# Seven block products in place of eight for the two first matrices of a feed-forward, with tokens stationary and the activations turned

## What is computed

```
h = rmsnorm(x, norm_ffn_g[layer])
x = x + (silu(h @ w1) * (h @ w3)) @ w2      # w1, w3: 1024 x 2816, w2: 2816 x 1024
```

## Time and profile before

| | |
|---|---|
| median of three runs | 2030.04 us |
| span of the profiled execution | 2026.6 us |
| TensorE matmul busy | 1956.4 us (97%) |
| TensorE weight load busy | 1243.3 us (61%) |
| VectorE busy | 466.4 us (23%) |
| ScalarE busy | 324.9 us (16%) |
| HBM read | 561.97 MB, 278 GB/s over the span |

### The profile page before, as it was taken

The page is one execution under the profiler, slowest core; times in us unless marked ns, Lnnn a source line. Parts: engine busy times, 40 slices in busy tenths (PEclk is TensorE's granted clock), DMA queues, the critical chain, the costliest instruction groups (busy, mean ns, idle before and its releaser), DMA issues.

```text
span 2026.6 us, 25597 instructions
## 1 busy us (share of the span) xinstructions
PE 1956.4 (97%) x10149; PEld 1243.3 (61%) x10150; DVE 466.4 (23%) x886; ACT 324.9 (16%) x686; POOL 28.9 (1%) x50
## 2 busy tenths in 40 slices
PE   7999899999999999999999999999999999999998
PEld 4866444433334444433333348788888899888887
DVE  1441311111011111101101123541101377410102
ACT  1231211111011111111101123421000120210001
POOL 2200000000000000000000000000000000000000
PEclk8999899999999999999999999999999999999999
DMA  9959499999989979999999996334444433344410
GB/s 354 307 184 376 185 395 421 422 422 422 422 337 420 421 311 420 422 422 422 422 421 422 422 351 199 104 105 145 160 151 147 144 113 110 118 140 160 150 42 22
DMA packets 170668, 563.94 MB, mean 278 GB/s; under 512 B 10758, under 2 KB 110376, under 8 KB 118128
## 3 DMA queue, kind: packets, MB, share of 16 engines
q1 hardware_dynamic: 167648, 554.96, 71.0%
q0 software_dynamic: 2192, 7.34, 1.3%
q10 hardware_dynamic: 768, 0.76, 0.1%
HBM read 561.97 MB, written 1.05 MB: 278 GB/s over the span
## 4 chain that ended last, share of the span: by engine, by line
PE 79%; DMA 14%; SPq 4%; DVE 1%; ACT 1%; issue 1%; DVEq 0%
PE psum L1173 15%; PE psum L809 15%; DMA ring<-in_w_dram 13%; PE psum L837 8%; PE psum L1145 7%; PE psum L1206 5%; PE psum L952 5%; SPq L418 4%; PE psum L659 4%; PE psum L588 3%; PE psum L780 2%; PE psum L796 2%; PE psum L1227 1%; PE psum L818 1%; DMA ring<-in_w_ada_dram 1%; PE psum L565 1%
## 5 line engine op out<-in xcount | busy, mean ns | idle before, releaser
L809 PE MATMUL psum<-ring,arena 128*64 128x512 f32 x2176 | 490.8, 596 | 38.4 <-DMA ring<-in_w_dram 38.4
L809 PEld LDWEIGHTS psum<-ring,arena 128*64 128x64 f32 x2176 | 151.9, 137 | 369.5 <-issue 252.8
L1173 PE MATMUL psum<-hT,ring 128*128 128x256 f32 x1408 | 307.5, 379 | 0.0
L1173 PEld LDWEIGHTS psum<-hT,ring 128*128 128x128 f32 x1408 | 267.5, 190 | 36.4
L837 PE MATMUL psum<-ring,arena 128*64 128x512 f32 x1088 | 241.7, 597 | 3.2
L1973 DVE TENSOR_SCALAR arena<-psum 128x512 f32<-128x512 f32 x34 | 23.5, 692 | 731.7 <-PE psum L818 731.7
L837 PEld LDWEIGHTS psum<-ring,arena 128*64 128x64 f32 x1088 | 77.7, 137 | 145.4 <-issue 145.4
L1145 PE MATMUL psum<-arena,ring 128*128 128x256 f32 x640 | 141.4, 379 | 0.0
L1145 PEld LDWEIGHTS psum<-arena,ring 128*128 128x128 f32 x640 | 121.6, 190 | 16.5
L1444 ACT ACTIVATE arena<-arena 128x512 f32<-128x512 f32 x34 | 21.4, 630 | 547.2 <-DVE arena L1973 547.1
L1206 PE MATMUL psum<-hT,ring 128*128 128x256 f32 x352 | 79.1, 379 | 0.0
(11 more groups left out here) (388 smaller groups left out, 1617.5 us busy)
## 6 DMA issues: line engine op xcount, KB each, us to landing
ring<-in_w_dram SPq DMA_DIRECT2D x384, 1024.0 KB, 22.6
ring<-in_ffn_w_dram SPq DMA_DIRECT2D x66, 1024.0 KB, 5.3
ring<-in_w_ada_dram SPq DMA_DIRECT2D x24, 1024.0 KB, 11.2
ring<-in_odd_w_in_dram SPq DMA_DIRECT2D x16, 1024.0 KB, 5.5
ring<-in_even_w_in_dram SPq DMA_DIRECT2D x13, 1024.0 KB, 12.7
ring<-in_w_in_dram SPq DMA_DIRECT2D x12, 1024.0 KB, 17.8
ring<-in_w_out_dram SPq DMA_DIRECT2D x4, 1024.0 KB, 14.7
ring<-in_even_w_out_dram SPq DMA_DIRECT2D x4, 1024.0 KB, 5.1
```

The costliest lines, as they stand in the source:

```text
L809: mm = nc.tensor.matmul(bank[4 + q][64 * h:64 * h + 64, :], xg[:, k, SLOTS * r:SLOTS * (r + 1)], ring[(C_MOE + k) % RING][:, (2 * h + q) * ...
L1173: mm = nc.tensor.matmul(bank[4 + 2 * (i % 2) + b][:, h * T:(h + 1) * T], cols(n)[:, k, h * P:(h + 1) * P], hT[:, k * T:(k + 1) * T], start ...
```

## The change

Let the 256 tokens be two blocks of 128 (rows of the product) and the 1024 channels two halves; w1's chunk is one column block of the weights, w3's the other, so a step is a product of a 2x2 by a 2x2 of blocks. It is now formed by Winograd's form of Strassen's algorithm, with seven products of blocks (`p1` to `p7`) where eight stood. With A11, A12 the halves of the first 128 tokens, A21, A22 of the second, and B11, B21 those of w1, B12, B22 of w3:

- four sums of activations, once a feed-forward, into the dead `mixT` (`ffn_x`): A21+A22, that less A11, A11-A21, A12 less the second;
- four sums of weights, in every step, 128x1024 each (`split_weights`): T1 = B12-B11, T2 = B22-T1, T3 = B22-B12, T4 = B21-T2, into one of two sets of buffers (`ffn_w`);
- seven products of 4 matmuls. The stationary operand is a 128x128 block of activations and 256 columns of weights (from the ring or `ffn_w`) move, so results have tokens as rows. P1 lies in bank 4, and ScalarE copies it (`ffn_kept`) before P2 is added in the same bank; P6, P7 and P4 add up in bank 5, P5 and P3 in bank 6;
- VectorE reads the banks between the products and adds P1 and its own sums: u2 (behind P6), u3 (behind P7), c22, c21 (behind P4), c12 (behind P3), 128x256 each;
- silu with the norm's factor as a scale for each row on ScalarE (two of 128x256), and the product with the linear half on VectorE (two SCALAR_TENSOR_TENSOR of 128x256);
- four transpositions in every step (`turn_hidden`) and a copy of 128x512 from bank 7 on ScalarE (`save_hidden`), since `down` still wants the activations turned.

`down` and the order of chunks stay. The norm's sums are now taken for each token (`column_sums`, four matmuls of one column a call). The weight sums of step 0 stand on VectorE ahead of the projection's additions, those of step 1 inside step 0 (behind c22), those of step i+1 at the head of step i for i from 1 to 9. Some semaphores were merged (`turned`, `turned_saved`), with shifted counts; that changes no order.

```
+                def turn_hidden(i):
+                    s = layer * FFN_STEPS + i
+                    pe.wait_ge(S.ffn_hidden, 2 * s + 2)
+                    pe.wait_ge(S.turned_saved, 2 * UNITS + s)
+                    for a in range(TT):
+                        for k in range(2):
+                            mm = nc.tensor.transpose(bank[7][:, k * T + a * P:k * T + (a + 1) * P],
+                                                     ffn_tok[a][:, k * P:(k + 1) * P], ident)
+                    mm.then_inc(S.turned, 1)
...
+                    def product(home, x, w, first, ready=None):
+                        for k in range(4):
...
+                            mm = nc.tensor.matmul(home, x[:, k, :], w[:, k, :], start=(first and k == 0), stop=(k == 3),
+                                                  skip_group_check=True)
...
+                    def p4():
+                        pe.wait_ge(S.ffn_split, split_at(s, "T4"))
+                        pe.wait_ge(S.ffn_sum, sum_at(s, "u3"))
+                        product(homes[1], x_blocks[:, 4:8, P:T], split[3], False).then_inc(S.ffn_part, 1)
...
+                    def p6():
+                        pe.wait_ge(S.ffn_split, split_at(s, "T2"))
+                        if i == 0:
+                            pe.wait_ge(S.ffn_split, mixed_at(layer, 4))
+                        else:
+                            pe.wait_ge(S.ffn_sum, sum_at(s - 1, "c21"))
+                        product(homes[1], ffn_x[1], split[1], True).then_inc(S.ffn_part, 1)
+
+                    def p7():
+                        pe.wait_ge(S.ffn_split, split_at(s, "T3"))
+                        pe.wait_ge(S.ffn_sum, sum_at(s, "u2"))
+                        product(homes[1], ffn_x[2], split[2], False).then_inc(S.ffn_part, 1)
+
+                    p1()
+                    if i == 0:
+                        p2()
+                    p6()
+                    p5()
+                    if i >= 1:
...
+                        turn_hidden(i - 1)
+                    p7()
+                    if i:
+                        p2()
+                    p4()
+                    p3()
...
-                        for b in range(2):
-                            arrived(n)
-                            for h in range(2):
-                                for k in range(KT):
...
-                                    mm = nc.tensor.matmul(bank[4 + 2 * (i % 2) + b][:, h * T:(h + 1) * T],
-                                                          cols(n)[:, k, h * P:(h + 1) * P], hT[:, k * T:(k + 1) * T],
-                                                          start=(k == 0), stop=(k == KT - 1))
...
+                V.tensor_tensor(t1, b12, b11, ALU.subtract).then_inc(S.ffn_split, 1)
+                dve.wait_ge(S.ffn_split, split_at(s, "T1"))
+                V.tensor_tensor(t2, b22, t1, ALU.subtract).then_inc(S.ffn_split, 1)
+                V.tensor_tensor(t3, b22, b12, ALU.subtract).then_inc(S.ffn_split, 1)
+                dve.wait_ge(S.ffn_split, split_at(s, "T2"))
+                V.tensor_tensor(t4, b21, t2, ALU.subtract).then_inc(S.ffn_split, 1)
...
+                    if 1 <= i < FFN_STEPS - 1:
+                        split_weights(first, layer, i + 1)
+                    dve.wait_ge(S.ffn_part, product_at(s, "P6"))
+                    dve.wait_ge(S.ffn_kept, s + 1)
+                    V.tensor_tensor(ffn_u2, b1, ffn_p1, ALU.add).then_inc(S.ffn_sum, 1)
+                    dve.wait_ge(S.ffn_part, product_at(s, "P7"))
+                    V.tensor_tensor(ffn_u3, b1, ffn_p1, ALU.add).then_inc(S.ffn_sum, 1)
+                    dve.wait_ge(S.ffn_sum, sum_at(s, "u3"))
+                    V.tensor_tensor(ffn_c22, b2, ffn_u3, ALU.add).then_inc(S.ffn_sum, 1)
+                    if i == 0:
+                        dve.wait_ge(S.root_ready, 4 + 2 * layer)
+                        V.reciprocal(ffn_r, ffn_r).then_inc(S.y_scale, 1)
+                        dve.wait_ge(S.y_scale, layer + 1)
+                        split_weights(first, layer, 1)
...
+            dve.wait_ge(S.nsa_out, UNITS)
+            dve.wait_ge(S.mix_ready, 3)
+            split_weights(C_FFN0, 0, 0)
             add_projection(C_EOUT, 30, 104)
-            inverse(3)
             ffn(C_FFN0, 0, 96, gained_6)
```

More of the change, by code:

```diff
@@ L115, with products_of, product_at, split_at @@
                          ("cmp_add", TT * N_CMP), ("cmp_keep", TT * N_CMP), ("levels", (LEVELS + 1) * P)])
+PRODUCTS = ("P1", "P6", "P5", "P7", "P2", "P4", "P3")
+FIRST_PRODUCTS = ("P1", "P2", "P6", "P5", "P7", "P4", "P3")
+SPLITS, SUMS = ("T1", "T2", "T3", "T4"), ("u2", "u3", "c22", "c21", "c12")
+def products_of(i):
+    return PRODUCTS if i else FIRST_PRODUCTS
+def product_at(s, name):
+    return 6 * s + products_of(s % FFN_STEPS).index(name) + 1
+def split_at(s, name):
+    return 4 * (s + (s >= 1) + (s > FFN_STEPS)) + SPLITS.index(name) + 1
+def mixed_at(layer, n):
+    return 4 * ((FFN_STEPS + 1) * layer + 1) + n
+def sum_at(s, name):
+    return 5 * s + SUMS.index(name) + 1
 def shape_constants():
@@ L568, in sum_squares, with column_sums @@
                     mm.then_inc(S.ssq_ready, 1)
+            def column_sums(i, q):
+                pe.wait_ge(S.sq_ready, 4 * i + q + 1)
+                for k in (2 * q, 2 * q + 1):
+                    for a in range(TT):
+                        mm = nc.tensor.matmul(bank[7][:, a:a + 1], sq[:, k * T + a * P:k * T + (a + 1) * P], ones[:, 0:1],
+                                              start=(k == 0 and a == 0), stop=(k == KT - 1), skip_group_check=True)
+                if q == 3:
+                    mm.then_inc(S.ssq_ready, 1)
             def project(n, j, src, parts, m=256):
@@ L1137, in down @@
                 def down(i):
+                    s = layer * FFN_STEPS + i
                     w = ring[n % RING][:, :].rearrange("p (k n) -> p k n", k=2)
                     arrived(n)
-                    pe.wait_ge(S.ffn_hidden, layer * FFN_STEPS + i + 1)
+                    pe.wait_ge(S.turned_saved, 2 * UNITS + s + 1)
                     if i < FFN_STEPS - 1:
                         for k in range(2):
+                            if k == 1 and i == FFN_STEPS - 2:
+                                turn_hidden(i + 1)
@@ L1160, in ffn @@
                     if i < FFN_STEPS:
[L1161 to L1164, removed]
[L1165 to L1177 removed]
+                        products(i)
+                        n += 2
                     if i >= 1:
@@ L1274, in _ @@
                 project(C_OOUT + j, 50 + j, mixT, "columns")
-                sum_squares(5, j - 1)
+                column_sums(5, j - 1)
             ffn(C_FFN1, 1)
@@ L1690, in _ @@
             squares(xT, S.proj_saved, 50)
-            root(5)
             ffn(1)
@@ L2152, in add_projection, with up_at @@
                     only_gained(j, col, hT)
[L2154 to L2165 removed]
+            def up_at(first, i):
+                return first + (3 * i - 1 if i else 0)
@@ new lines, in split_weights @@
+            def split_weights(first, layer, i):
+                s, n = layer * FFN_STEPS + i, up_at(first, i)
+                for at in (n, n + 1):
+                    dve.wait_ge(landed[at % RING], 16 * (at // RING + 1 + E_N))
+                (b11, b21), (b12, b22) = ([ring[at % RING][:, 1024 * j:1024 * j + 1024].rearrange("p (k n) -> p k n", k=4)
+                                           for j in range(2)] for at in (n, n + 1))
+                t1, t2, t3, t4 = ffn_w[i % 2]
+                V.tensor_tensor(t1, b12, b11, ALU.subtract).then_inc(S.ffn_split, 1)
[4 more added lines that the diff above has]
+                V.tensor_tensor(t4, b21, t2, ALU.subtract).then_inc(S.ffn_split, 1)
@@ L2260, in _ @@
                                        in1=hg_g[:, pair, :], op0=ALU.mult, op1=ALU.mult).then_inc(S.mix_ready, 1)
+            dve.wait_ge(S.mix_ready, 7)
+            split_weights(C_FFN1, 1, 0)
             add_projection(C_OOUT, 50, 112)
-            inverse(5)
             ffn(C_FFN1, 1, 120, hT)
```

162 lines of the change are left out of this document (120 added, 42 removed).

## The result

| | before | changed |
|---|---|---|
| median | 2030.43 us (4 runs, 2027.58 to 2034.72) | 2014.26 us (4 runs, 2010.36 to 2017.89) |
| ratio | | 0.9912, 95% interval 0.9889 to 0.9935 |
| span of the profiled execution | 2026.6 us | 2009.0 us |

The changed kernel is faster by 16.2 us at the median and by 17.6 us of span; forecast were 17.5 us and 2012.5 us. The interval lies wholly beyond 0.2%.

What follows compares the result with a forecast made beforehand. TensorE's instruction count was taken to bound the feed-forward. Matmuls removed -38.0, transpositions +10.3, norm's sums 0 and stops +10.2 gave -17.5 us, from 2030.04 to 2012.5 us, with 2007 to 2022 for 8 in 10.

Steps and rivals of the forecast that it cites:

- What bounds it: Feed-forward: TensorE, busy 97% of the span, sets the time by instruction count times 0.4317 us, plus its stops.
- the matmuls removed: First matmuls of each feed-forward step: 28 instead of 32, 1.727 us a step, 38.0 us less over 22 steps.
- Transpositions: Four added on TensorE in every feed-forward step: 0.47 us a step, 10.3 us more over 22 steps.
- Norm's sums: Column sums on TensorE, now by token: 0.4 us less at most over eight calls, taken as 0.
- ends and heads of the layers: Step 0's weight sums ahead of the layers: 0.3 us late at most, hidden; end of a feed-forward: no stop.
- The steady step: Feed-forward steps 2 to 9: no stop of TensorE, 19.46 us a step, next u2 in time by 3.8 us.
- Steps 0 and 1: Stops before P4 of step 0, P6 and P7 of step 1: 0.9, 1.0, 3.2 us; 10.2 us more in all.
- the clock's: Rival, 17%: TensorE's clock falls at the 3.2 us stop, costing 1.7 to 5 us a feed-forward; say 2019 us.
- Exposed weight loads: Rival, 8%: nine heads a step each expose a 0.19 us weight load, 37.6 us more: 2050.1 us.
- Cheaper sums: Rival, 9%: VectorE's sums are cheaper or overlap better, so only the 0.9 us stops stay: 2004.0 us.
- Dearer sums: Rival, 8%: VectorE's sums are slower beside DMA and TensorE; at twice the price 20.2 us more, 2032.7 us.
- The sum: Whole kernel: matmuls, transpositions, norm's sums and stops together give 17.5 us less, 2012.5 us.

Runs made afterwards that it cites:

- the version without stops: Changed kernel with weight sums of steps 1 and 2 moved, column sums ahead of P2, step 0's P5 split around P7: 2004.73 us, ratio 0.9865 to before.
- eight-product kernel: Against the kernel before: tokens stationary, results turned by four transpositions, norm by token, all eight products, no sums of activations or weights; ratio 1.0053.
- the changed kernel again: The changed kernel, unaltered, run once more against the kernel before: ratio 0.9904, median 2015.13 us of 6 runs.

## Why the prediction was right

**What bounds it, and the matmuls removed:** right. 38.0 us follow from the pace of 0.216 us a pass, which stayed, and the account of the version without stops closes to 0.1 us.

**Transpositions:** 0.45 us a group by the eight-product kernel, 9.9 us in all for the 10.3 forecast from the earlier trace rows.

**Norm's sums, ends and heads of the layers:** nothing, as forecast. In layer 0 VectorE added the first part of the projection at once behind its weight sums, in layer 1 with 0.73 us to spare, and the stretch between the feed-forwards is 190.26 us for 190.25.

**The steady step:** right, 19.43 us for 19.46, no stop, and slack before u2 of 4.35 us where I had reckoned 3.8.

**Steps 0 and 1:** the place and the cause were right, the sizes a little off. Forecast were 0.9, 1.0 and 3.2 us; measured 0.77, 0.39 and 2.57. Too dear was VectorE's group of weight sums, 4.67 us for 5.06, since I put 0.04 us between operations that in fact overlap by 0.08; two groups in a row make 0.8 us of it. Too dear was the handover to TensorE as well: the prediction put 0.25 us, with a weight load of 0.19 in it that nothing hides, and P4 and P7 start 0.15 and 0.14 us behind the record that they wait for (u3's ends at 1385.09, u2's at 1397.29). The load's record does not lie ahead of P7's matmul (1397.43) but starts with it:

```profile
1397.40 1.78 PEld L1205 LDWEIGHTS psum<-arena,mixT 128*128 128x128 f32 x5 [2.62 <-DVE arena L2321]
```

One stop was missed: P2 of step 0 follows P1 at once and must wait 0.7 us for ScalarE's copy out of the shared bank. In the steady step 5.65 us of other work lie between P1 and P2; in step 0 nothing does, and the prediction did not ask again there. The errors cancel in part: 4.45 us a feed-forward for 5.1, or 4.7 with the slightly longer work behind the stops (212.55 less 207.83).

**The rivals:** the clock's came true in part. I gave it 17% and priced it at 1.7 to 5 us a feed-forward; it fell in the first alone and cost 1.54 us (214.09 less 212.55). A granted clock under 1.00 behind the stop of step 1, one of the prediction's signs of being wrong, was there: 0.72. The Trainium skill (TensorE: Matmul & The Clock Gate, HAM oscillation) warns that idle gaps of TensorE let its clock fall to half, and the trace agrees in that; the gaps in its example, waits for DMA of 3 to 5 us, are longer than the 2.4 us that were followed by a fall here. Exposed weight loads: fallen, since with nine heads in a step that begin with a wait the passes stay at 0.216 us. Cheaper sums: true to 0.39 us a group, not to the half that it needed. Dearer sums: fallen.

**The sum**, by the measured sizes: -38.0 + 9.9 + 2 x 4.7 + 1.5 = -17.2, against 17.1 measured in the feed-forwards and 17.6 in the span. That this is so near the forecast 17.5 is in part luck: the stops came out 0.8 us below their 10.2, the transpositions 0.4 below theirs, and the fall of the clock, which the sum did not hold, took 1.5. What stays open is why the clock fell in the first feed-forward of all four profiles and in the second of none, behind stops of the same length; where in the span the stop lies differed by up to 11 us among those profiles. The medians came to 16.2, 20.8 and 14.8 us apart in the three groups of runs. Equal kernels differ by as much: beside `the changed kernel again`, the kernel before took 2025.67 us at a mean granted clock of 0.994 and 2038.97 at 0.987. The changed kernel's three profiles span 2009.0, 2014.2 and 2019.9 us, and the mark lies at 1195.2, 1198.3 and 1206.2 us: most of the difference lies ahead of it, where the granted clock differed (0.95, 0.91 and 0.86 from 200 to 300 us). Why it did, and whether this sets the medians apart, is not shown.

## What to carry to other kernels

Where an engine is full and another is a quarter busy, count the first's instructions and check each new wait against its clock; but do it for the first rounds of a loop apart, whose order and cover differ from the steady ones: here all of TensorE's standing sat there, and moving two groups of weight sums, one call of column sums and half a product got 11 us back. Work for the idle engine belongs where the full one runs on something that needs none of it, even a stage earlier. Compare executions stage by stage from a common mark when stages that were not touched differ by more than the effect.

## What the runs showed of the hardware

- A stop of TensorE of 2.4 us was followed by the lower granted clock (1.2 GHz) in five cases of ten, one of 2.8 us in 16 of 16 and one of 4.9 us in two of two; a fall cost 1.5 to 1.8 us behind the first two kinds. After the two single stops of 0.9 us none was seen.
- At a wait that is met in time a product's head costs nothing: a steady step with nine heads takes 19.43 us, which is 44 x 0.4317 + 0.44. At one that is not, TensorE's next matmul starts 0.14 to 0.15 us behind the end of VectorE's record, and its weight load's record starts 0.03 us before it.
- Two independent 128x1024 operations of VectorE start 1.14 us apart though each record is 1.22 us long; where the second reads the first's result it is 1.25.
- A transposition of 128x128 in float32 costs TensorE 0.11 us in a stream of matmuls, a quarter of a float32 matmul of 256 columns, and a one-column matmul 0.20 us with its two loads.
